# One GpSimd operation for the three scaled copies of a turned tile, and sums of squares once a chunk, in the scan of a hybrid RG-LRU, SSD and PEER block

## What is computed

```
xdt = xs * dt[..., None]
cb = einsum('bclgn,bcsgn->bgcls', cm, bm)
y_diag = einsum('bghcls,bcsghp->bclghp', cb[:, :, None] * decay_ls, xdt)
states = einsum('bclgn,bclghp->bcghpn', bm, xdt * decay_states[..., None])
# over the chunks: prev = the state before the chunk, state = chunk_decay * state + states
y_off = einsum('bclgn,bcghpn->bclghp', cm, prev) * decay_out[..., None]
y = y_diag + y_off + xs * d_skip
yg = (y * silu(z)).reshape(bsz, seqlen, G, SSD_INNER // G)
y = rms_norm(yg, norm_w)        # needs the sum of squares of each token and group
```

## Time and profile before

| what | value |
|---|---|
| time, median of 3 runs | 4144.43 us (4143.16 to 4147.24) |
| the profiled execution's own time | 4141.22 us |
| its span in the trace | 4139.5 us |
| the scan's steps in the trace | from 881.3 us (first L821) to 1062.1 us (end of the last gate) |
| PE busy over the span | 3899.4 us (94%) |
| DVE, ACT, POOL busy over the span | 2544.7, 1692.7, 1793.9 us |

### The profile page before, as it was taken

How to read it: one execution, slowest core, us unless ns; L and a number is a source line. 1 busy time by engine, 2 the same in 40 slices (tenths; PEclk the granted TensorE clock), 3 DMA queues, 4 the chain that set the end, 5 groups by cost and what they waited for, 6 DMA issues and landing times. The chain is left out here.

```text
span 4139.5 us, 58970 instructions
## 1 busy us (share of the span) xinstructions
PE 3899.4 (94%) x21728; PEld 3215.5 (78%) x21728; DVE 2544.7 (61%) x4787; ACT 1692.7 (41%) x3248; POOL 1793.9 (43%) x1275
## 2 busy tenths in 40 slices
PE   8899999989899969898999999999969999999998
PEld 4688888856677769888999899999947767777666
DVE  3455411148775326688999899987765555555555
ACT  2123343368422431126777777777512222222222
POOL 0333333359445112133333333345466666666664
PEclk9999999999999989999999999999989999999999
DMA  7222323358566332177888888899999989999997
GB/s 306 53 83 96 99 94 102 106 179 273 165 193 187 102 121 62 46 262 233 267 266 277 257 276 269 275 295 360 360 334 330 329 319 343 330 332 329 325 327 281
DMA packets 639576, 956.53 MB, mean 231 GB/s; under 512 B 198996, under 2 KB 416740, under 8 KB 638436
## 3 DMA queue, kind: packets, MB, share of 16 engines
q1 hardware_dynamic: 319492, 423.09, 31.2%
q0 software_dynamic: 110592, 402.70, 27.7%
q10 hardware_dynamic: 209248, 127.55, 9.9%
HBM read 807.33 MB, written 145.88 MB: 230 GB/s over the span
## 5 line engine op out<-in xcount | busy, mean ns | idle before, releaser
L1909 POOL DMA_INDIRECT down_rows<-in_peer_down_dram,row_ids x384 | 457.0, 1190 | 850.9 <-DVE row_u L2049 761.9
L1930 PE MATMUL p_u<-h2T_hi,downT_hi 128*128 128x320 f32 x2048 | 656.8, 321 | 11.4 <-ACT gelu_out L1980 11.4
L1930 PE MATMUL p_u<-h2T_lo,downT_hi 128*128 128x320 f32 x2048 | 636.8, 311 | 0.0
L1930 PE MATMUL p_u<-h2T_hi,downT_lo 128*128 128x320 f32 x2048 | 636.2, 311 | 0.0
L2049 DVE CUSTOM_DVE_ANT_0 gate_rows<-down_rows,x_tok_rows 128x1024 f32<-128x1024 f32 x384 | 469.2, 1222 | 86.1 <-DMA down_rows<-in_peer_down_dram,row_ids 69.2
L2205 POOL DMA_INDIRECT up_rows<-in_peer_up_dram,row_ids_turned x384 | 417.2, 1086 | 240.8 <-PE p_rows L2368 145.8
L2407 PE MATMUL p_y<-up_hi,coef_hi 128*128 128x512 f32 x1240 | 494.8, 399 | 1.1 <-DVE coef_lo L2302 1.1
L2407 PE MATMUL p_y<-up_lo,coef_hi 128*128 128x512 f32 x1240 | 485.5, 392 | 0.0
L2407 PE MATMUL p_y<-up_hi,coef_lo 128*128 128x512 f32 x1240 | 482.7, 389 | 0.0
L2312 DVE TENSOR_TENSOR y_acc<-p_y,y_acc 128x512 f32<-128x512 f32 x310 | 211.3, 690 | 372.9 <-PE p_y L2407 338.4
L517 PE MATMUL p<-hT_hi,w_hi 128*128 128x512 f32 x1024 | 405.1, 396 | 0.0
(11 more groups left out here) (351 smaller groups left out, 7918.6 us busy)
## 6 DMA issues: line engine op xcount, KB each, us to landing
down_raw<-in_peer_down_dram SPq DMA_DIRECT2D x128, 512.0 KB
up_raw<-in_peer_up_dram SPq DMA_DIRECT2D x128, 512.0 KB
scratch_gu<-gelu_out ACTq DMA_DIRECT2D x128, 320.0 KB
gelu_in<-scratch_gu SPq DMA_DIRECT2D x128, 320.0 KB
weights_in<-scratch_w SPq DMA_DIRECT2D x128, 320.0 KB
w_raw<-in_w_in_dram SPq DMA_DIRECT2D x64, 512.0 KB
w_ada_sb<-in_w_ada_dram SPq DMA_DIRECT2D x12, 2048.0 KB, 14.6
scratch_w<-weights_out ACTq DMA_DIRECT2D x40, 512.0 KB
```

The costliest lines, as they stand in the source:

```text
L1909: pool.indirect_dma_start(out=rows[:, c % RING, :], out_offset=None, in_=inp["peer_down"][0], in_offset=bass.IndirectOffsetOnAxis(ap=row_i ...
L1930: mm = pe.matmul(ps_u[half][:, 0:HD], d[:, n % 3, k, :], h2[h][:, k, half * HD:(half + 1) * HD], start=(j == 0), stop=(j == 3 * KD - 1))
```

## The change

GpSimd makes the three copies in one operation. `x_scaled` has room for three copies of 512 columns side by side, for each of two buffers; `x_factors` holds for each chunk and head the three factors (dt, dt times decay, D), made once ahead of the loop. The operation reads `x_tok` three times (an outer stride of zero) and a factor for 64 columns each, and writes 128x1536. One semaphore, `scaled_done`, takes the place of three. The waits of the three operations stand together ahead of the one.

The sums of squares are taken once a chunk. `y_sq` keeps four tiles for each of two chunks, and `squares(c)` makes four products with 512 columns (the four groups' 128 tokens side by side) in place of four times four with 128. `keep_sum(c)` copies 128x512 at once. `square_of` is made each step as before.

```diff
-        xdt = m.sb(st, "x_dt", [P, 2, W])
-        xdd = m.sb(st, "x_dt_decay", [P, 2, W])
-        x_d = m.sb(st, "x_skip", [P, 2, W])
+        scaled = m.sb(st, "x_scaled", [P, 2, 3, W])
+        factor = m.sb(st, "x_factors", [P, 3, CH, SH])
+        xdt, xdd, x_d = (scaled[:, :, f] for f in range(3))
...
+                pool.tensor_copy(factor[:, 0], dt_all).then_inc(factors_ready, 1)
+                pool.tensor_tensor(factor[:, 1], dt_all, dec_state, ALU.mult).then_inc(factors_ready, 1)
+                pool.tensor_copy(factor[:, 2], d_row[:].unsqueeze(1).to_broadcast([P, CH, SH])).then_inc(factors_ready, 1)
+                pool.wait_ge(factors_ready, 3)
...
                     pool.wait_ge(xt_done, n + 1)
                     if n >= 2:
                         pool.wait_ge(y_done, n - 1)
-                    pool.tensor_tensor(heads(xdt[:, v]), heads(xt[:, v]), per_head(dt_all, n), ALU.mult).then_inc(xdt_done, 1)
-                    pool.wait_ge(xdt_done, n + 1)
-                    if n >= 2:
                         pool.wait_ge(state_mm, n - 1)
-                    pool.tensor_tensor(heads(xdd[:, v]), heads(xdt[:, v]), per_head(dec_state, n), ALU.mult
-                                       ).then_inc(xdd_done, 1)
-                    if n >= 2:
                         pool.wait_ge(yo_done, 2 * (n - 1))
-                    pool.tensor_tensor(heads(x_d[:, v]), heads(xt[:, v]),
-                                       d_row[:, g * SHG:(g + 1) * SHG].unsqueeze(2).to_broadcast([P, SHG, SP_]),
-                                       ALU.mult).then_inc(skip_done, 1)
+                    pool.tensor_tensor(scaled[:, v].rearrange("p f (h q) -> p f h q", q=SP_),
+                                       heads(xt[:, v]).unsqueeze(1).to_broadcast([P, 3, SHG, SP_]),
+                                       factor[:, :, c, g * SHG:(g + 1) * SHG].unsqueeze(3).to_broadcast([P, 3, SHG, SP_]),
+                                       ALU.mult).then_inc(scaled_done, 1)
...
-                def squares(n):
+                def squares(c):
 
-                    pe.wait_ge(sq_done, n + 1)
-                    if n >= 1:
-                        pe.wait_ge(ss_kept, n)
+                    pe.wait_ge(sq_done, (c + 1) * SG)
+                    if c >= 1:
+                        pe.wait_ge(ss_kept, c)
                     for j in range(WT):
-                        mm = pe.matmul(ps_q[:, 0:P], ones[:], sq[:, n % 2, j * P:(j + 1) * P],
-                                       start=(j == 0), stop=(j == WT - 1))
+                        mm = pe.matmul(ps_q[:].rearrange("p (g t) -> p g t", t=P), ones[:],
+                                       sq[:, c % 2, :, j * P:(j + 1) * P], start=(j == 0), stop=(j == WT - 1))
                     mm.then_inc(ss_done, 1)
...
-                    if n >= 2:
-                        squares(n - 2)
-                squares(STEPS - 1)
+                    if n >= SG + 1 and n % SG == 1:
+                        squares(n // SG - 1)
+                squares(CH - 1)
...
-                def keep_sum(n):
-                    c, g = divmod(n, SG)
-                    act.wait_ge(ss_done, n + 1)
-                    act.copy(ss_all[:, g, c * P:(c + 1) * P], ps_q[:, 0:P]).then_inc(ss_kept, 1)
+                def keep_sum(c):
+                    act.wait_ge(ss_done, c + 1)
+                    act.copy(ss_all[:, :, c * P:(c + 1) * P], ps_q[:].rearrange("p (g t) -> p g t", t=P)).then_inc(ss_kept, 1)
...
-                    if n >= 2:
-                        keep_sum(n - 2)
+                    if n >= SG + 2 and n % SG == 2:
+                        keep_sum(n // SG - 1)
                 square_of(STEPS - 1)
-                keep_sum(STEPS - 2)
-                keep_sum(STEPS - 1)
+                keep_sum(CH - 1)
```

More of the change, by code:

```diff
@@ L737, in ssd @@
         yo = m.sb(st, "y_tok", [P, 2, W])
-        sq = m.sb(st, "y_sq", [P, 2, W])
+        sq = m.sb(st, "y_sq", [P, 2, SG, W])
         y_ch = m.sb(st, "y_chunk", [P, 2, SI // P, P])
@@ L759, in ssd @@
         cb_kept, m_done, yg_done = m.sem("cb_causal_done"), m.sem("cb_decay_done"), m.sem("y_gated")
-        xdt_done, xdd_done, skip_done, dec_done = (m.sem(f"ssd_{n}") for n in ("x_dt", "x_dt_decay", "x_skip", "state_dec"))
+        factors_ready, scaled_done, dec_done = (m.sem(f"ssd_{n}") for n in ("factors", "x_scaled", "state_dec"))
         y_stored = [m.sem(f"y_stored{i}") for i in range(2)]
@@ L814, in _ @@
                 pool.memset(state[:], 0.0).then_inc(state_zero, 1)
+                pool.tensor_copy(factor[:, 0], dt_all).then_inc(factors_ready, 1)
+                pool.tensor_tensor(factor[:, 1], dt_all, dec_state, ALU.mult).then_inc(factors_ready, 1)
+                pool.tensor_copy(factor[:, 2], d_row[:].unsqueeze(1).to_broadcast([P, CH, SH])).then_inc(factors_ready, 1)
+                pool.wait_ge(factors_ready, 3)
                 pool.wait_ge(state_zero, 1)
                 for n in range(STEPS):
-                    v, g = n % 2, n % SG
+                    v = n % 2
+                    c, g = divmod(n, SG)
                     pool.wait_ge(xt_done, n + 1)
@@ L873, in multiply @@
                     pe.wait_ge(bt_done, n + 1)
-                    pe.wait_ge(xdd_done, n + 1)
+                    pe.wait_ge(scaled_done, n + 1)
                     if n >= 1:
@@ L936, in square_of @@
                     act.wait_ge(yg_done, n + 1)
-                    if n >= 2:
-                        act.wait_ge(ss_done, n - 1)
-                    act.activation(sq[:, n % 2].rearrange("p (k t) -> p k t", t=P), y_ch[:, of_chunk(n), tiles(n), :],
+                    if n >= 2 * SG and n % SG == 0:
+                        act.wait_ge(ss_done, n // SG - 1)
+                    act.activation(sq[:, of_chunk(n), n % SG].rearrange("p (k t) -> p k t", t=P), y_ch[:, of_chunk(n), tiles(n), :],
                                    ACT.Square).then_inc(sq_done, 1)
-                def keep_sum(n):
-                    c, g = divmod(n, SG)
-                    act.wait_ge(ss_done, n + 1)
-                    act.copy(ss_all[:, g, c * P:(c + 1) * P], ps_q[:, 0:P]).then_inc(ss_kept, 1)
+                def keep_sum(c):
+                    act.wait_ge(ss_done, c + 1)
+                    act.copy(ss_all[:, :, c * P:(c + 1) * P], ps_q[:].rearrange("p (g t) -> p g t", t=P)).then_inc(ss_kept, 1)
                 decay(0)
@@ L951, in _ @@
                     if n >= 2:
-                        act.wait_ge(xdt_done, n - 1)
-                        act.wait_ge(skip_done, n - 1)
+                        act.wait_ge(scaled_done, n - 1)
                     act.copy(xt[:, v], ps_x[:]).then_inc(xt_done, 1)
@@ L973, in add_up @@
                     dve.wait_ge(yo_done, 2 * n + 1)
-                    dve.wait_ge(skip_done, n + 1)
+                    dve.wait_ge(scaled_done, n + 1)
                     dve.tensor_tensor(yo[:, v], yo[:, v], x_d[:, v], ALU.add).then_inc(yo_done, 1)
```

## The result

The changed kernel takes 4162.48 us (median of 5 runs, 4161.7 to 4164.79), against 4144.43 us for the kernel before (4140.9 to 4147.8, 5 runs). The ratio is 1.0044, with a 95% interval from 1.0029 to 1.0058: slower by 18 us, more than the spread of the runs explains. The profiled execution has a span of 4163.1 us, 23.6 over that of before.

What follows compares the result with a forecast made beforehand. The prediction took the loop of cb_decay and GpSimd operations excluding each other to bound the scan at 5.58 us a step. Terms of 3.7, 17.5 and 0.8 gave +22 us on 4144.4, forecast as 4167, range 4150 to 4187.

Steps and rivals of the forecast that it cites:

- 31 ordinary excesses: Over the scan's 31 steps, each ordinary step was to be 0.12 us longer than before, 3.7 us in all.
- seven chunks: In each of 7 chunks, squares add 2.00 us and the large copy of sums 0.50, 17.5 us in all.
- What bounds the scan: In the scan before the change, cb_decay and GpSimd's two-input SBUF operations wait for each other, setting 5.58 us a step.
- S: Length of the one GpSimd operation x_scaled with 1536 columns, taken as 2.80 us.
- The ordinary step: A scan step without the products of squares: S + 2.90 = 5.70 us, 0.12 over the 5.58 before.
- The step with the squares: The scan step holding a chunk's four products of squares: 7.70 us, 2.00 over an ordinary step; the one behind 6.20.
- The lump: A chunk's four products of squares on TensorE in one go: 3.44 us, ahead of the next turn of x.
- The end: Behind the last gate, the last squares and sums take 4.94 us against 4.1 for the store: +0.8 us.
- the lock doesn't bind: Rival, chance 0.08: in the scan VectorE needn't wait for the whole GpSimd operation; -12 to -15 us, 4131.
- The lump does not hide: Denies the rival, chance 0.12, that the scan's products of squares in one go cost no time: +8 us, 4152.
- GpSimd does not keep its turn into `state_dec`: Denies a rival, chance 0.17 shared with a slower S: VectorE also waits through L834, 1.04 us in 24 steps, +47.
- The clock did not fall: Denies the rival, chance 0.02, that TensorE's clock drops to its 1.2 GHz level in the scan: above 4220 us.

Runs made afterwards that it cites:

- e8: The kernel before with only the masked C times B (cb_causal) moved from SBUF to PSUM: 4130.2 us against 4146.0, ratio 0.9967.
- e9: e1 with a fourth copy that nothing reads, 128x2048 in place of 128x1536: 4178.3 us against 4143.1 for the kernel before, ratio 1.0079.
- e1: The changed kernel with the sums of squares back in every step, so the one GpSimd operation alone: 4153.0 us against 4146.0 before, ratio 1.0022.
- e3: The changed kernel with the masked C times B (cb_causal) in PSUM instead of SBUF: 4136.3 us against 4146.0 for the kernel before, ratio 0.9974.
- e6: e1 with the one GpSimd operation cut by factor into three of 512 columns: 4141.1 us against 4146.0 for the kernel before, ratio 0.9987.
- e5: e4 with the masked C times B (cb_causal) in PSUM: 4133.0 us against 4146.0 for the kernel before, ratio 0.9967.
- e2: The kernel before with only the sums of squares once a chunk, three GpSimd operations kept: 4157.9 us against 4146.0, ratio 1.0032.
- e4: The changed kernel with the four products of squares spread, one a step: 4147.3 us against 4146.0 for the kernel before, ratio 1.0001.

## Why the prediction was right

The forecast was 4167 us and slower; it is 4162.5. By the profiled executions it was +22 and came out at +23.6; in the scan itself +22 against +21.8 + 0.3. By the medians it is +18, inside the interval of +12 to +24. (The sum gives 4166.4 for a median; 4167 is rounded up.) The phases behind the scan took 3071 to 3080 us in the twelve traces, with no edit in them, so a few microseconds between one profiled execution and a median carry no cause.

That the scan fits to a few tenths is in part luck. The 31 ordinary excesses came to 31 x 0.08 = 2.5 us where 3.7 was forecast, the seven chunks to 7 x 2.63 = 18.4 for 17.5. The rest, +0.9, was in no term: the first gate comes 1.4 us later behind the memset and the first step is 1.2 longer, and the last step is 1.5 shorter. The steps themselves, 5.66, 7.80 and 6.15 for 5.70, 7.70 and 6.20, are the better witness.

*What bounds the scan.* The loop of `cb_decay` and GpSimd's operations was read right: e8 takes away that one meeting and the step falls from 5.58 to 5.14, with TensorE busy throughout. Busy shares of 94% and 97% both misled here; neither engine set the 5.58 alone.

*S.* Taken at 2.80, measured 2.76. The broadcast factor's rate was the right row, not the plain one: 2.76 for 1536 and 3.62 for 2048 columns (e9) make 1.68 ns a column and 0.18 us fixed. The estimate of 3.33 us, from the rate in the Trainium skill ("GPSIMD Engine Reference", the section on performance against the Vector engine), was too high by a fifth for an operand of this kind. By the Trainium skill's "SBUF — State Buffer", the section on who interferes with whom, a vector operation with two inputs in SBUF and a GpSimd one that reads SBUF exclude each other for a whole instruction, and a vector operation with at most one input in SBUF, outside the modes that take two ports, does not contend. These runs agree: `cb_decay` waits to the end of an operation of 2.76 and of 3.62 us (e1, e9), and not at all when its second input is in PSUM (e3, e8). Between two operations VectorE got its turn in the scan (e6), but not always in the last phase.

*The ordinary step.* S + 2.90 gave 5.70; measured 5.66, with S 0.04 shorter. That the whole of S is in the loop is shown by e9, and that it is there through `cb_decay` by e3.

*The step with the squares.* 7.70 forecast, 7.80 measured; 6.20 and 6.15 for the one behind. The tenth is the one that e5 shows: the passes take 3.54, where I had 3.44, since the first of them takes 0.10 longer than the row of L867 told. e2 has 7.69 with the three operations. The lump is the larger part: in the pieces tried alone, +14.9 of the scan for the squares (e2) and +7.7 for the operation (e1), together 22.6, for 21.8 with both. Part of e1's is the small copy of sums each step, which the changed kernel doesn't have; with the squares spread the operation costs 3.1 (e4). So with the operation in place the lump and its large copy cost 213.1 - 194.4 = 18.7 us.

*The end.* +0.8 forecast, +0.3 measured: the term was mis-sized. The sum took the store as done 4.1 us behind the last gate. But where the last sum is late, the next phase starts 1.20 behind it (5.04 and 6.24 here; 5.58 and 6.78 in e4), and before it started at 5.92, so the slack went to 4.72 behind the gate. Little hangs on it. The setup of the factors (0.72, 0.40 and 0.40 us) is hidden as said.

*The rivals.* That the lock doesn't bind is refuted by every `cb_decay` of 2.8 us; its price, -12 to -15, was not tested. e3 frees `cb_decay` alone and gives -8 in the scan and -10 in the medians; its chunk takes 21.35 us where the rival had 20.7, and some 0.5 of the difference is the step in which L972 still waits for GpSimd. The lump does not hide. GpSimd does not keep its turn into `state_dec`. The clock did not fall.

## What to carry to other kernels

Fewer and longer operations are no gain in themselves on an engine that shares its way into memory with another: in this scan the other lost the rest of whichever operation it met, so three operations of a third of the length can be faster than one, and putting one operand into PSUM can be worth more than either. Work that is cheaper in one piece has to stand where the engines that wait behind it can spare the whole piece: four products of 512 columns take 3.54 us in place of 4 x 1.00, which saves 0.12 us a step on average, and cost 2.1 us once a chunk where they stand ahead of the next step's inputs. And a busy share near 100% on one of two engines that exclude each other may be the waiting of one inside the other.

## What was not expected of the hardware

A GpSimd product with a factor broadcast over 64 columns runs at 1.68 ns a column from 1536 to 2048 columns, and a difference of two plain inputs, written as fp32r, at 2.20 ns. Which of these things makes the difference wasn't tried. The first pass of squares behind L887 takes 0.10 us longer than the passes behind it, whether it has 128 columns (0.21 for 0.11, the kernel before) or 512 (0.53 for 0.43, e5 and the changed kernel).
